# The residual x of the output projection, transposed by the transfer engines during the second branch's gates and kept in DRAM

## The chip, the cores and the metric

The kernel runs on one core of a Trainium2 chip. The metric is the device time of one execution in microseconds; less is better. The core has a matrix engine (TensorE, PE in the profile), a vector engine (VectorE, DVE), a scalar engine (ScalarE, ACT), a general engine (GpSimd, POOL), and SyncE (SP), which here only issues transfers. Transfers are carried out by 16 DMA engines.

## What is computed

One layer of a hybrid encoder, for 1024 prompt tokens and 32 sample tokens (1056 in all), width 1024, everything in 32-bit floats. Cut to what matters here:

```python
h = rmsnorm(x, norm_mix)
(a_b, a_c, a_x, qb, kb, vb, qc, kc, vc, qi, ki, wi, g_a, g_b, g_c) = split(h @ w_in)
br_a = (a_b * causal_dwconv(a_c * a_x)) @ w_a_out      # branch 1: gated convolution
br_b = window_attention(qb, kb, vb) @ w_swa_o          # branch 2
br_c = sparse_attention(qc, kc, vc, qi, ki, wi) @ w_dsa_o   # branch 3: top-k keys
merged = sigmoid(g_a) * br_a + sigmoid(g_b) * br_b + sigmoid(g_c) * br_c
x = x + merged @ w_out                                 # the residual that is changed
x = x + conv_ffn(rmsnorm(x, norm_ffn))                 # w_gate, w_up, w_down
y = rmsnorm(x, norm_final)
```

## The kernel before

Activations lie in SBUF with the channels on the 128 partitions and the 1056 tokens along the row ("columns"); a tile is 128 channels. To reach the accuracy of 32-bit floats, every matrix product is made of three products of rounded halves: high weights by high values, high weights by low values, low weights by high values. ACT makes the high part of a weight tile (`w_hi`, line 2240 is the helper that copies), DVE or POOL the low part (`w_lo`). A *job* is the product of one 128-column tile of weights with all tokens: 8 token tiles of nine matmuls each (line 1602), or 4 where the input is only 512 wide. The jobs are numbered in the order in which PE runs them; each uses one of two weight slots and one of two groups of PSUM banks, so the weights of job n are split when job n-2 is done.

All waits are written by hand with semaphores; each engine has its own instruction stream and runs it in order. SP's stream issues nearly all transfers, so a wait in it holds up every transfer behind it.

**The gates of the second branch** (jobs from `J_GB` on; `gate_loads` for SP, `gates` for ACT, DVE and PE). After the window attention, a loop of eight passes runs, two jobs a pass: a gate tile (8 token tiles; ACT takes its tanh, line 2466) and a tile of the branch's projection (4 token tiles). Beside them SP loads the gate weights of the third branch into `gate_w_raw`, ACT and POOL split them, and `gate_store` writes the two parts to DRAM, from where the sparse attention reads them later. In a pass SP waits for `lo_ready` before it loads w_in's tile for the gate job two ahead of the running ones, for `gate_lo` before `gate_store`, then loads the tile of w_swa_o, then the next `gate_w_raw`.

**The output projection** (jobs `J_WO` and `J_WO` + 1, then `out_product`). Before it, the eight jobs of the third branch's projection are merged: DVE multiplies with the gates, which lie where the residual will be (`GATES` and `X2` both start at SBUF unit 0), adds, and counts `sum_ready`; ACT and DVE make `merged_hi` and `merged_lo`. Output tiles 0 and 1 are plain jobs. Tiles 2 to 7 are made in three pairs by a scheme of seven half-sized products instead of eight (A11, S1, S2, S4, S3, A12, A22), each 24 matmuls of 264 columns (line 2009). They need sums and differences of quarters of the weights (`out_sum`, line 3653, DVE), their high parts (`out_hi`, ACT) and low parts (`out_lo`, line 3659, DVE), and mixes of the merged halves (`merged_mix`, lines 3620 to 3636, DVE; their high parts by ACT, line 2667). DVE adds each product to the residual `X2` (line 3668, `out_add`), for tiles 0 and 1 whole (line 3672, `residual`). PE waits for some of these additions before it starts a product in the same banks.

The residual has to be in columns, but x comes in rows. Before, SP loads x again in rows (`x_rows_again`, lines 1130 to 1133) when the third branch's last product is done, PE transposes it with 72 identity products (`x_tile`, eight after each of nine token tiles of jobs `J_WO` and `J_WO` + 1, into banks 6 and 7), and ACT evicts each set into `X2` (`xr_out`). DVE waits for all nine evictions ahead of `residual(0)`. Behind the loads of x, SP loads w_out's columns for pair 1 (line 1142), the second half of them once job `J_WO` + 1's weights are split.

## Time and profile before

| | us |
|---|---|
| median of the runs | 1749.39 |
| the runs | 1749.38, 1749.39, 1750.65 |
| span of the profiled execution | 1748.6 |
| PE busy | 1717.8 |
| DVE busy | 1341.5 |
| ACT busy | 757.8 |
| POOL busy | 579.4 |

The span goes from the first to the last instruction of one profiled execution; the median is of executions without the profiler, and lies 0.8 us above it. Starts in the rows below are microseconds from the start of that span. An instruction's duration includes its latency, so that the next one on the same engine can start a little before it ends: DVE's operations on 512 or 528 elements last 0.68 to 0.70 us and follow each other by 0.60 to 0.62, those on 1056 elements by 1.17.

### The profile page before, as it was taken

To read this page: it belongs to the slowest core of one execution; us is meant where nothing else is said; L and a number is where in the kernel's file an instruction comes from. 1 tells how busy PE (TensorE), PEld (TensorE's weight loads), DVE (VectorE), ACT (ScalarE), POOL (GpSimd) and SP (SyncE) were. 2 spreads that over 40 slices of the span, in tenths; PEclk is the share of its full clock that TensorE was granted. 3 is DMA by queue.
4 is the path that set the end of the run, shared out by engine and by line. 5 is a ranking of instruction groups with operands and counts; after the bars stand their busy time and mean duration, and the time that the engine had idled before them with its cause. 6 is when DMAs were issued, how large, how long until landed. Compare 5 with 4: busy or idle time off the path is not lost.

```text
span 1748.6 us, 32318 instructions
## 1 busy us (share of the span) xinstructions
PE 1717.8 (98%) x12275; PEld 1678.6 (96%) x12275; DVE 1341.5 (77%) x2193; ACT 757.8 (43%) x1333; POOL 579.4 (33%) x466
## 2 busy tenths in 40 slices
PE   6999999999999999999999999999999999999998
PEld 6999999999999999888899999999999999999998
DVE  6689899978799996778759989666666665865765
ACT  5344333368621234767734563333333333422334
POOL 2211842266745431000021102655455554121130
PEclk9999999999999999999999999999999999999999
DMA  4101111111243415422324112222222223533112
GB/s 157 49 25 43 49 43 48 49 38 28 68 137 124 128 40 171 144 85 85 109 71 151 49 49 61 87 85 75 74 80 80 87 74 111 167 117 112 61 37 100
DMA packets 179190, 146.43 MB, mean 84 GB/s; under 512 B 10140, under 2 KB 149676, under 8 KB 179052
## 3 DMA queue, kind: packets, MB, share of 16 engines
q1 hardware_dynamic: 178076, 142.54, 26.3%
q0 software_dynamic: 976, 2.00, 0.5%
q8 instruction: 93, 1.52, 0.4%
q14 instruction: 45, 0.37, 0.1%
HBM read 118.22 MB, written 26.28 MB: 83 GB/s over the span
## 4 chain that ended last, share of the span: by engine, by line
PE 91%; DVE 4%; ACT 2%; issue 1%; DMA 1%; POOL 1%; SPq 0%; DVEq 0%; ACTq 0%; POOLq 0%
PE ps L1602 28%; PE ps L2079 23%; PE ps L2152 7%; PE ps L2138 7%; PE ps L1714 5%; PE ps L1775 4%; PE ps L1795 4%; PE ps L1614 4%; PE ps L2009 3%; PE ps L1921 3%; PE ps L1869 1%; PE ps L1632 1%; PE ps L1876 1%; ACT probs L2537 0%; DMA x_rows<-in_x_prompt 0%
## 5 line engine op out<-in xcount | busy, mean ns | idle before, releaser
L3171 DVE MAX8 top<-key_mask 128x8 f32<-128x1024 f32 (+5 forms) x166 | 151.8, 917 | 9.7 <-DVE key_mask L3171 3.4
L1602 PE MATMUL ps<-h_hi,w_hi 128*128 128x352 f32 (+1 forms) x720 | 158.0, 327 | 0.0
L1602 PE MATMUL ps<-h_hi,w_lo 128*128 128x352 f32 (+1 forms) x720 | 155.2, 323 | 0.0
L1602 PE MATMUL ps<-h_lo,w_hi 128*128 128x352 f32 (+1 forms) x720 | 154.8, 323 | 0.0
L1289 POOL TENSOR_TENSOR w_lo<-w_raw,w_hi 128x512 fp32r<-128x512 f32 (+1 forms) x43 | 79.3, 1843 | 217.4 <-ACT w_hi L2240 217.3
L3171 DVE MATCH_REPLACE8 key_mask<-top,key_mask 128x1024 f32<-128x1024 f32 (+5 forms) x166 | 149.4, 904 | 0.3 <-issue 0.3
L2079 PE MATMUL ps<-mix_hi,quarter_hi 128*128 128x264 f32 x672 | 136.9, 285 | 0.2 <-ACT x_one L2240 0.2
L2079 PE MATMUL ps<-mix_hi,quarter_lo 128*128 128x264 f32 x672 | 136.4, 284 | 0.0
L2079 PE MATMUL ps<-mix_lo,quarter_hi 128*128 128x264 f32 x672 | 136.0, 284 | 0.0
L1602 PEld LDWEIGHTS ps<-h_hi,w_hi 128*128 128x128 f32 (+1 forms) x720 | 120.6, 187 | 2.6 <-issue 0.9
L1602 PEld LDWEIGHTS ps<-h_hi,w_lo 128*128 128x128 f32 (+1 forms) x720 | 122.5, 186 | 0.5
L1602 PEld LDWEIGHTS ps<-h_lo,w_hi 128*128 128x128 f32 (+1 forms) x720 | 121.5, 186 | 0.5
L2240 ACT ACTIVATE w_hi<-w_raw 128x1024 fp32r<-128x1024 f32 (+3 forms) x88 | 65.7, 749 | 125.6 <-PE ps L2138 56.5
L3800 DVE TENSOR_TENSOR quarter_lo<-sum,quarter_hi 128x512 fp32r<-128x512 f32 x84 | 71.1, 864 | 59.4 <-ACT quarter_hi L2240 59.1
L2079 PEld LDWEIGHTS ps<-mix_hi,quarter_hi 128*128 128x128 f32 x672 | 104.4, 189 | 0.6 <-ACT x_one L2240 0.4
L2079 PEld LDWEIGHTS ps<-mix_lo,quarter_hi 128*128 128x128 f32 x672 | 104.2, 188 | 0.0
L2079 PEld LDWEIGHTS ps<-mix_hi,quarter_lo 128*128 128x128 f32 x672 | 103.9, 188 | 0.0
L2079 PE MATMUL ps<-h_hi,quarter_lo 128*128 128x264 f32 x504 | 103.1, 286 | 0.0
L2079 PE MATMUL ps<-h_hi,quarter_hi 128*128 128x264 f32 x504 | 102.5, 285 | 0.6 <-ACT z_one L2240 0.6
L2079 PE MATMUL ps<-h_lo,quarter_hi 128*128 128x264 f32 x504 | 102.7, 285 | 0.0
L3512 DVE TENSOR_TENSOR probs_t_lo<-ps,probs_t_hi 128x512 fp32r<-128x512 f32 (+1 forms) x112 | 71.9, 642 | 33.1 <-ACT probs_t_hi L2240 32.0
L2240 ACT ACTIVATE quarter_hi<-sum 128x512 fp32r<-128x512 f32 x84 | 50.1, 626 | 89.7 <-POOL sum L1516 49.4
(452 smaller groups left out, 5017.5 us busy)
## 6 DMA issues: line engine op xcount, KB each, us to landing
w_raw<-in_w_in SPq DMA_DIRECT2D x54, 256.0 KB, 3.0
w_hi<-gate_highs SPq DMA_DIRECT2D x48, 256.0 KB, 2.8
w_lo<-gate_lows SPq DMA_DIRECT2D x48, 256.0 KB, 3.0
ffn_tiles<-t SPq DMA_DIRECT2D x44, 264.0 KB, 2.4
w_raw<-in_w_gate SPq DMA_DIRECT2D x44, 256.0 KB, 3.1
w_raw<-in_w_up SPq DMA_DIRECT2D x44, 256.0 KB, 3.1
w_raw_in_lo<-in_w_in SPq DMA_DIRECT2D x30, 256.0 KB, 3.0
w_raw<-in_w_down SPq DMA_DIRECT2D x32, 192.0 KB, 2.8
```

The costliest lines, as they stand in the source:

```text
L1289: nc.gpsimd.tensor_tensor(WLO[:, k, 0:tiles, :], raw[:, k, 0:tiles, :], WHI[:, k, 0:tiles, :].bitcast(F32), ALU.subtract).then_inc(lo_read ...
L1602: last = nc.tensor.matmul(PS[0:rows, NB * k + b, 0:e - a], w[:, k, t, 0:rows], x[:, t, a:e], start=m == 0 and w is WHI and x is hi, stop=m ...
L1614: last = nc.tensor.transpose(out, in_, IDENT[p0:p0 + r, p0:p0 + r])
L1714: last = nc.tensor.matmul(PS[:, 2 * bank + b, 0:QP], a_slot(w, n)[:, t, :], x[:, tile + t, at + b * QP:at + (b + 1) * QP], start=first and ...
L1775: last = nc.tensor.matmul(piece_bank(q), wt[:, w % 2, t, :], piece_at(x, t, p), start=t == 0 and wt is WHI and x is H_HI, stop=t == KT - 1 ...
L2079: last = nc.tensor.matmul(PS[:, 2 * pair + b, 0:QP], w[:, t * P:(t + 1) * P], x[:, tile + t, a:a + QP], start=first and t == 0 and w is WQ ...
L2138: last = nc.tensor.matmul(PS[:, NB * k + b, 0:PIECE], w[:, k, t, :], x[:, b * PIECE:(b + 1) * PIECE], start=t == 0 and w is WHI and x is F ...
L2152: last = nc.tensor.matmul(PS[:, 2 * pair + b, 0:QP], w[:, t * P:(t + 1) * P], x(t, b * QP, (b + 1) * QP), start=first and t == 0 and w is ...
L2240: return nc.scalar.activation(out, in_, ACT.Copy)
L3171: step.mark(V_.max(top, s) if find else V_.match_replace(s, top, s, TAKEN))
L3512: V_.tensor_tensor(PT_LO[:, q % 2, 0:n], PS[:, 4 + q % 2, 0:n], PT_HI[:, q % 2, 0:n].bitcast(F32), ALU.subtract).then_inc(pt_lo, 1)
L3800: V_.tensor_tensor(WQ_LO[q][:, :], src, WQ_HI[q][:, :].bitcast(F32), ALU.subtract).then_inc(q_lo_ready, 1)
```

## The change

The rows of x aren't loaded again. x, seen as 16-bit words, is a matrix with 2048 columns; channel c is its columns 2c and 2c + 1. In pass j of the gates loop SP issues two transposing transfers (prompt and sample) of 256 such columns, from DRAM into `X_TURNED`, 128 partitions by 2 by 1056 words; `x_bounce` writes that to DRAM so that each of the 256 columns is a row there; `x_plane_load` reads it back with the two halves of one channel in one partition (`X_PLANES`); ACT copies it so that the halves of each token lie side by side, which makes the 32-bit words of 128 channels of x in columns (`X_COLUMNS`); `x_store` writes this tile to DRAM. At the output projection SP waits for the last merge and for the stores, and loads the eight tiles straight into `X2`; DVE waits for them (two tiles a semaphore) before it adds. The transposes, the evictions and the waits for them go.

The diff, cut:

```diff
@@ SBUF and DRAM @@
-        XR = place("x_rows_again", [P, NT + 1, D], F32, 24)
+        X_TURNED = place("x_halves_turned", [P, 2, TOK], U16, 38)
+        X_PLANES = place("x_half_planes", [P, 2, TOK], U16, 39)
+        X_COLUMNS = place("x_columns", [P, TOK], F32, 40)
...
+        X_HALVES = nc.dram_tensor("x_halves", (2 * D, TOK), U16, kind="Internal").ap()
+        X_TILES = nc.dram_tensor("x_tiles", (KT, P, TOK), F32, kind="Internal").ap()
@@ SP @@
+            def x_turn(j):
+                at = bass.ds(j * (2 * P), 2 * P)
+                sp.dma_start_transpose(X_TURNED[:, :, 0:SEQ], x_halves(ins["x_prompt"])[:, at]).then_inc(xt_turned, 16)
+                sp.dma_start_transpose(X_TURNED[:, :, SEQ:TOK], x_halves(ins["x_sample"])[:, at]).then_inc(xt_turned, 16)
+            def x_bounce(j):
+                at = bass.ds(j * (2 * P), 2 * P)
+                sp.wait_ge(xt_turned, 32 * j + 32)
+                apart(sp)
+                sp.dma_start(X_HALVES[at, :].rearrange("(c p) t -> p c t", p=P), X_TURNED[:, :, :]).then_inc(xt_halves, 16)
+            def x_plane_load(j):
+                at = bass.ds(j * (2 * P), 2 * P)
+                sp.wait_ge(xt_halves, 16 * j + 16)
+                apart(sp)
+                sp.dma_start(X_PLANES[:, :, :], X_HALVES[at, :].rearrange("(p h) t -> p h t", h=2)).then_inc(xt_planes, 16)
+            def x_store(j):
+                sp.wait_ge(xt_columns, landed(j + 1))
+                apart(sp)
+                sp.dma_start(X_TILES[bass.ds(j, 1), :, :].rearrange("a p t -> p (a t)"), X_COLUMNS[:, :]).then_inc(xt_stored, 16)
@@ SP, gate_loads @@
                 sp.dma_start(GATE_RAW[:, :, :], columns(w_in, C_G + 2 * D)).then_inc(sparse_raw, 16)
+                sp.wait_ge(pv_done, WINDOW[-1]["q"] + len(WINDOW[-1]["chunks"]))
+                x_turn(0)
+                x_bounce(0)
+                x_plane_load(0)
                 with sp.Fori(1, KT) as j:
+                    x_turn(j)
                     free(n0, j, 0)
                     load(0, plain(0, w_in[:, :, bass.ds(j * P + (C_G + gate * D), P)]))
                     gate_store(j - 1)
+                    x_bounce(j)
+                    x_store(j - 1)
                     free(n0, j, 1)
                     load(1, split(j))
+                    x_plane_load(j)
                     sp.wait_ge(gates_stored, 32 * j)
@@ SP, attention_loads @@
                 if n0 == J_C:
+                    x_store(KT - 1)
                     gate_store(KT - 1)
@@ SP, output projection @@
             sp.wait_ge(job_done, J_WO - 1)
-            for i in range(0, NT, 2):
-                src = ins["x_prompt"][0, i * P:(i + 2) * P, :].rearrange("(t p) d -> p t d", p=P)
-                sp.dma_start(XR[:, i:i + 2, :], src).then_inc(xr_in[i // 2], 16)
-            sp.dma_start(XR[0:DEC, NT, :], x_rows(NT)).then_inc(xr_in[NT // 2], 16)
+            sp.wait_ge(sum_ready, KT)
+            sp.wait_ge(xt_stored, landed(16 * KT))
+            for j in range(KT):
+                sp.dma_start(X2[:, j, :], X_TILES[j]).then_inc(xr_in[j // 2], 16)
@@ PE @@
-            project(J_WO, 0, 0, M_HI, M_LO, ready=(m_lo, 0), order=SPARSE_ORDER,
-                    between={t: x_tile(t - 3) for t in range(3, KT)})
-            project(J_WO, 0, 1, M_HI, M_LO, between={t: x_tile(t + 5) for t in range(4)})
+            project(J_WO, 0, 0, M_HI, M_LO, ready=(m_lo, 0), order=SPARSE_ORDER)
+            project(J_WO, 0, 1, M_HI, M_LO)
...
-                if m == 1:
-                    pe.wait_ge(xr_out, NT + 1)
-                else:
+                if m > 1:
                     pe.wait_ge(added, out_count(1, Q_S4 if m == 2 else Q_A22))
@@ ACT, gates @@
                     following(n0, j, 1)
+                    act.wait_ge(xt_planes, landed(16 * j + 16))
+                    act.wait_ge(xt_stored, landed(16 * j))
+                    apart(act)
+                    copy(X_COLUMNS[:, :].bitcast(U16).rearrange("p (t h) -> p t h", h=2),
+                         X_PLANES[:, :, :].rearrange("p h t -> p t h")).then_inc(xt_columns, 1)
@@ ACT, attention_jobs @@
+                if n0 == J_C:
+                    act.wait_ge(xt_stored, landed(16 * KT))
@@ ACT, output projection @@
-            for i in range(NT + 1):
-                r = rows_of(i)
-                act.wait_ge(xr_t, i + 1)
-                src = PS[:, 6:8, :].rearrange("p b (j t) -> p (b j) t", t=P)
-                copy(X2[:, :, i * P:i * P + r], src[:, :, 0:r]).then_inc(xr_out, 1)
@@ DVE @@
+                if q in (Q_A11, Q_S1, Q_S2):
+                    dve.wait_ge(xr_in[m], 32)
...
                 done(J_WO, 0, k)
+                dve.wait_ge(xr_in[0], 32)
...
-            dve.wait_ge(xr_out, 5)
             mix_t_raw(4)
-            dve.wait_ge(xr_out, NT + 1)
```

## Rows read from the trace of the kernel before

**Rows 1.** The page's first part: busy us, share of the span, instructions.

```profile
PE 1717.8 (98%) x12275; PEld 1678.6 (96%) x12275; DVE 1341.5 (77%) x2193; ACT 757.8 (43%) x1333; POOL 579.4 (33%) x466
```

**Rows 2.** Instructions on x_rows_again: duration in ns min/median/max, first and last start.

```profile
L1614 PE MATMUL ps<-ident,x_rows_again x72: 221/272/273, 942.4 to 961.6; 128*128 128x128 f32 x64, 32*128 32x32 f32 x8
```

**Rows 3.** Timeline of PE: start us, us, line, operation, count [idle before <-releaser].

```profile
936.59 0.65 PE L1602 MATMUL ps<-merged_hi,w_hi 128*128 128x352 f32 x3
...
942.41 1.04 PE L1614 MATMUL ps<-ident,x_rows_again 128*128 128x128 f32 x8
...
967.64 0.41 PE L2009 MATMUL ps<-merged_hi,out_hi 128*128 128x264 f32 x2
```

**Rows 4.** Timeline of ACT, last eviction of x.

```profile
961.82 0.39 ACT L2240 ACTIVATE residual<-ps 128x256 f32<-128x256 f32 x1 [1.02 <-PE ps L1614]
```

**Rows 5.** Timeline of DVE from the last merge on.

```profile
938.23 1.26 DVE L3401 TENSOR_TENSOR conv_in<-merge_sum,t 128x1056 f32<-128x1056 f32 x1
...
953.67 0.68 DVE L3653 TENSOR_TENSOR out_sum<-w_raw 128x512 f32<-128x512 f32 x1
...
958.80 2.56 DVE L3636 TENSOR_TENSOR merged_mix<-merged_mix,merged_lo 128x528 f32<-128x528 f32 x4
...
962.24 1.26 DVE L3672 TENSOR_TENSOR residual<-ps,residual 128x1056 f32<-128x1056 f32 x1 [0.88 <-ACT residual L2240]
...
963.41 0.68 DVE L3659 TENSOR_TENSOR out_lo<-w_raw,out_hi 128x512 fp32r<-128x512 f32 x1
...
969.01 2.55 DVE L3623 TENSOR_TENSOR merged_mix_lo<-merged_mix,merged_mix_hi 128x528 fp32r<-128x528 f32 x2
...
982.46 0.71 DVE L3668 TENSOR_TENSOR residual<-ps,residual 128x528 f32<-128x528 f32 x1 [0.55 <-PE ps L2009]
```

**Rows 6.** Timelines of POOL and PE: differences of residual, a wait.

```profile
967.88 3.11 POOL L1497 TENSOR_TENSOR mix<-residual 128x528 f32<-128x528 f32 x2 [33.26 <-PE ps L1602]
...
994.43 0.51 PE L2009 MATMUL ps<-merged_mix_hi,out_hi 128*128 128x264 f32 x2 [0.30 <-DVE residual L3668]
```

**Rows 7.** SP's queue; stretches: length, busy PE PEld DVE ACT POOL, PEclk, DMA, GB/s.

```profile
936.79 2.08 SPq L1132 DMA_DIRECT2D x_rows_again<-in_x_prompt  x4
...
944.00:946.00 2.00, 2.00 (x17) 1.99 (x16) 1.83 (x4) 0.69 (x2) 0.00 (x0) 1.00 1.03 424
...
953.00:954.00 1.00, 1.00 (x8) 0.97 (x7) 1.00 (x3) 0.83 (x1) 0.00 (x0) 1.00 0.00 0
```

**Rows 8.** A stretch of the opening, columns as in rows 7.

```profile
16.00:20.00 4.00, 2.67 (x17) 2.46 (x17) 3.86 (x8) 2.66 (x4) 0.69 (x1) 0.68 0.78 180
```

**Rows 9.** Gates loop: a stretch as in rows 7, timelines of ACT, POOL, PE.

```profile
498.00:516.00 18.00, 18.00 (x113) 18.00 (x112) 16.58 (x26) 3.58 (x4) 8.54 (x4) 1.00 0.46 145
...
482.12 1.05 ACT L2240 ACTIVATE w_hi<-w_raw 128x1024 fp32r<-128x1024 f32 x1
...
486.92 0.63 ACT L2240 ACTIVATE w_hi<-w_raw 128x512 fp32r<-128x512 f32 x1 [3.75 <-PE ps L1602]
...
483.25 2.41 POOL L1289 TENSOR_TENSOR w_lo<-w_raw,w_hi 128x1024 fp32r<-128x1024 f32 x1 [6.58 <-ACT w_hi L2240]
...
486.72 0.65 PE L1602 MATMUL ps<-h_hi,w_hi 128*128 128x352 f32 x3
```

**Rows 10.** SP's queue, PE; issues with count, KB each, us to landing.

```profile
462.76 0.94 SPq L1007 DMA_DIRECT2D w_raw<-in_w_in  x2
...
468.87 0.28 PE L1921 MATMUL ps<-probs_t_lo,v_parts 128*128 128x256 f32 x1
...
gate_w_raw<-in_w_in SPq DMA_DIRECT2D x1, 512.0 KB, 3.8
...
gate_highs<-gate_w_hi SPq DMA_DIRECT2D x1, 512.0 KB, 2.7
```

**Rows 11.** Stretches as in rows 7: w_in's load; the store of idx_k_rows.

```profile
465.00:466.00 1.00, 1.00 (x10) 1.00 (x9) 0.00 (x0) 0.26 (x2) 1.00 (x2) 1.00 1.15 344
...
152.20:152.40 0.20, 0.20 (x4) 0.20 (x3) 0.20 (x1) 0.00 (x0) 0.00 (x0) 1.00 0.96 205
```

More of the change, by code:

```diff
@@ L1983, in _ @@
                 project(0, n // 2, n % 2, O_HI, O_LO, tiles=CT, pieces=ROUNDS)
-            def x_tile(i):
-                def run():
-                    pe.wait_ge(xr_in[i // 2], 16)
-                    pe.wait_ge(xr_out, i)
-                    r = rows_of(i)
-                    for j in range(KT):
-                        transpose(PS[:, 6 + j // 4, (j % 4) * P:(j % 4) * P + r],
-                                  XR[0:r, i, j * P:(j + 1) * P], xr_t if j == KT - 1 else None)
-                return run
-            project(J_WO, 0, 0, M_HI, M_LO, ready=(m_lo, 0), order=SPARSE_ORDER,
-                    between={t: x_tile(t - 3) for t in range(3, KT)})
-            project(J_WO, 0, 1, M_HI, M_LO, between={t: x_tile(t + 5) for t in range(4)})
+            project(J_WO, 0, 0, M_HI, M_LO, ready=(m_lo, 0), order=SPARSE_ORDER)
+            project(J_WO, 0, 1, M_HI, M_LO)
             def out_product(m, q, hi, lo, first=False, mix=None):
```

7 lines of the change are left out of this document (5 added, 2 removed).

## Prediction

> **What bounds the kernel now.** I read the page first. TensorE is busy 98% of the span [rows 1], so whatever takes time from PE with the other engines ready moves the end one for one, and so does whatever makes it wait. Busy shares can't tell which stretches have no second limit, so I read the two places the change touches: the output projection (936 to 994 us) in the timelines of PE, ACT, DVE and SP's queue, and the loop over the second branch's gates (461 to 606 us), where PE is busy 18.00 of every 18 us [rows 9].
>
> **Part 1: what leaves PE and ACT.** The 72 transposes of x [rows 2] go. They stand between groups of nine matmuls: the first four tiles of job 0 have none behind them and take 942.41 - 936.59 = 5.82 us, 1.455 each; jobs 0 and 1 together last from 936.59 to 967.64 = 31.05 us; sixteen tiles alone are 4 x 5.82 = 23.28 [rows 3]. PE loses 7.8 us and reaches the end of job 1 at 959.9. That is the ceiling, 0.44% of the span. ACT's nine evictions of x go too; ACT idled ahead of each, 1.02 us before the last [rows 4].
>
> **Part 2: DVE takes over.** The first product after job 1 (A11 of pair 1) needs its low weights (line 3659). In DVE's timeline its work from the merges on is an unbroken string up to 958.80 + 2.56 = 961.36; then 0.88 us of waiting for ACT's last eviction, residual(0) at 962.24, low weights at 963.41 [rows 5]. None of this string waits for the transposes except those 0.88 us, and DVE loses no instruction. Freed, it starts residual(0) at 961.36 and finishes A11's low part at 961.36 + 1.17 + 0.68 = 963.2: PE, there at 959.9, idles 3.3 us. Further on: PE needs A11's addition (line 3668) before product S2. DVE does from 963.2: low S1 0.60, five mixes 3.1, residual(1) 1.17, two mixes 1.2, low S2 0.60, the addition 0.69 = 970.6, and 1.2 us more where POOL's differences double the mixes behind residual(1) (969.01: 2.55 for two, while at 958.80 four of that size took 2.56; POOL's pair began at 967.88) [rows 5, 6]: 971.9. S2 could start then at best, against 973.5 before (967.64 and two products of 2.93 us). The same string holds PE today: at 994.43, before S2 of pair 2, it waited 0.30 us for an addition of DVE [rows 6], and from 945 to there DVE idled 0.88 and 0.55 us only (the second ends at 982.46) [rows 5]. So of the 7.8 us at most 0.88 + 0.55 + some tenths, 1.5 to 2.3 us, can come through. After 994 DVE waits for PE again; what is left there is kept.
>
> **Part 3: the late loads take that back.** The x loads went out from 936.79 on, w_out's for pair 1 behind them on the same queue, which ran at 424 GB/s with DMA share 1.03 and was empty by 953 [rows 7]: 4.3 MB of x and 1.05 MB of weights. DVE's weight sums (line 3653) began at 953.67, some 0.8 us later. The changed loads write over the gates, so SP waits for the last merge: 938.23 + 1.26 = 939.49 [rows 5]. They go out at 939.6, 2.8 us later, with the same bytes; the weights land near 955.7. DVE, ready at 953.67, waits 2.0 us. Residual(0) starts at 961.36 + 2.0 = 963.4 instead of 962.24, PE idles 959.9 to 965.3 (5.4 us), the chain arrives at 982 some 1.1 us late, the 0.55 us wait there absorbs half, and S2 of pair 2 starts about 0.5 us later than 994.43. Term of this stage: **+0.5 us**, bounds -2.3 (loads hidden) and +1.5 (the stored tiles flow a tenth slower than x's rows). The new waits of DVE for x tiles 0 and 1 end near 944 and cost nothing.
>
> **The clock in that gap.** In the opening, where PE was busy 2.67 of 4 us, its granted clock was 0.68 in the mean, so part of that stretch ran at the lower level, 1.2 GHz [rows 8]. A gap of 5.4 us may do the same: a product of 2.93 us (24 matmuls of 264 columns) would take 5.9 then. But S2 waits for DVE until about 973.9, while A11 and S1 need PE to 971.2 only, so 2.7 us of it are covered; I add nothing to the likeliest case, up to 1.5 us to the range. The Trainium skill (TensorE: Matmul & The Clock Gate, "Why this matters for your kernels") says that an idle gap between bursts puts the clock back to its lower level; the opening of this trace agrees.
>
> **Part 4: the gates loop.** Each of eight passes gains two transposing loads of together 540 KB, a store, a load and a store of 540 KB each, and an ACT copy. The copy has 2 x 1056 elements, at 1.05 us for 1024 [rows 9] 2.1 us; ACT idles 3.75 us before its next split [rows 9]: 0. The traffic, 2.16 MB in a pass of twelve tiles (12 x 1.455 = 17.46 us), adds 124 to 145 GB/s; the DMA share is 0.46 [rows 9]: 0 by itself. What counts is SP's order. The new wait for the last product of the window attention stands ahead of everything from pass 1 on. That product runs at 468.87 and ends by 469.2; today w_in's load for pass 1 leaves at 462.76 [rows 10]. Call X the time in which 540 KB flow transposed. From 469.25: fixed part of a load 2.3 (3.8 for gate_w_raw's 512 KB [rows 10] less 1.5 at 344 GB/s [rows 11]), X, the small second load 0.3: turned at 471.85 + X. Store 2.7 (gate_highs' landing [rows 10]): 474.6 + X. The plane load takes 2.0 to flow and 1.4 in flow: 478 + X; the next pass's transposes stand behind it until 478 + 2X, then w_in's 512 KB, 1.5: **479.5 + 2X**. ACT wants it at 482.12, POOL's 2.41 us end at 485.66, PE wants it at 486.72: 1.06 us spare, so due at 483.15 [rows 9, 10]. PE loses 2X - 3.65. X is not in this trace. From below: 1.3 us at the 424 GB/s of x's rows [rows 7] and 1.6 at the 344 of w_in's 512-byte pieces [rows 11]: no loss. The store of idx_k_rows, in 256-byte pieces, ran at 205 [rows 11]; if a transpose reads 128 columns of 16 bits at a time, its pieces are as long: X = 2.6, loss 1.6 us. From above: 205 GB/s is 20 ns for each such piece on one of 16 engines; if it were cut into 32-byte pieces (16 tokens of one column), X = 17,000 x 20 ns / 16 = 21 us. I take 2.6, the row with the nearest pieces: **+1.6 us**.
>
> The Trainium skill (Advanced Engine Details and Errata, "X-Bar Transpose (TRN2)") has transposing loads as fast as others, 350 to 400 GB/s; DMA: Bandwidth & Descriptors, "Latency and other measured facts", has 261 GB/s with a non-contiguous middle dimension. X would be 1.5 or 2.1 and this term 0 or 0.5, an estimate from those pages; no run here shows it yet.
>
> From pass 2 on SP waits for ACT's copy, 4.1 us after the tanh (split 2.0, copy 2.1), before w_b's load, whose job starts 11.6 us later (0). Then plane load (issued 7.0 after the tanh), gate_w_raw, transposes and w_in queue up: 7.0 + 2.0 + 1.4 + 1.5 + X + 1.5 + 0.5, due 17.46 + 2.0 after it: hidden up to X = 5.6. The last x_store holds up gate_store and the next attention's ACT, both of whose readers come a job of 11.6 us later: 0.
>
> **Sum.** The profiled span is 1748.6, 0.8 us under the median of the runs, 1749.39. 1749.4 + 0.5 + 1.6 = **1751.4**.
>
> **Rivals.** (a) Transposes are slow: X above 3.3 us makes the first pass lose over 3 us, with the +0.5 over 0.2%. X = 4.5 gives 5.4 + 0.5: 1755.3. For it: the small pieces, the 21 us above. Against: the rows at 344 and 205. Chance 0.27 for X up to 5.6. (a') Slower still: X = 7 gives 10.4 in the first pass and 7 x 1.4 = 9.8 in the others: 1770; 0.13. (b) They flow like plain loads, X under 1.7, and the w_out loads are late: +0.5, 1749.9. 0.15. At 350 to 400 GB/s the Trainium skill's page (Advanced Engine Details and Errata) leads here. (c) The loads of part 3 are hidden too, DVE's string alone bounds: 1749.4 - 2.0 = 1747.4; 0.08. (d) DVE doesn't bind and the whole 7.8 comes through: 1741.6; against it stands the unbroken string. 0.05. The likeliest case, X from 1.7 to 3.3, holds 0.32; its own range is 1749.5 to 1753.
>
> **How the numbers follow.** A measurement of this kernel can tell about 0.2%, 3.5 us, from no change. Faster 0.05; slower 0.40; within 0.55. The range leaves out (d), most of (c), and X above 6: low 1748.0, high 1762 (X = 5.8: 8.0 + 1.4 + 0.5 + clock 1.5 = 1760.8, rounded up).
>
> **What would show it.** Right: PE idle some 5 us before line 2009's first product, DVE idle 2 us before line 3653, residual(0) at the same distance from the last merge as worked out; PE idle at the third job of the gates loop only, for w_lo of that job, and ACT's w_hi there waiting for a DMA; transposes landing 4.5 to 5.5 us after issue. Wrong: a PE gap at the projection under 3 us (part 3), landings over 6 us or a gap in each pass (part 4), or a clock below 1.00 for longer than the gap. A stall of PE in another stage would overthrow the sum.

## The result, and the profile after

The changed kernel takes 1756.84 us, the median of five runs (1756.74 to 1758.49), where the kernel before took 1749.86 beside it: a ratio of 1.0039, interval 1.0028 to 1.0049. The change makes the kernel some 7 us slower. The forecast was 1751.4 in a range of 1748.0 to 1762.0; the range held, the likeliest case (1749.5 to 1753) did not. The time and a loss of over 3 us in the first pass of the gates loop are those of rival (a); whether its reason held too is asked further down.

First the page's first part and the opening of its second, to be read against [rows 1]:

```profile
span 1755.0 us, 32315 instructions
PE 1713.7 (98%) x12203; PEld 1674.2 (95%) x12203; DVE 1344.6 (77%) x2193; ACT 766.5 (44%) x1332; POOL 583.6 (33%) x466
```

PE lost its 72 instructions and 4.1 us of busy time, and the span grew by 6.4 us. ACT has 8.7 us more (eight copies of 2.2 us less nine evictions). So PE must wait longer. The list of PE's waits says where (waiting engine and line, what it waited for: us in total, times, longest):

```profile
PE ps L2043 <- DVE out_lo L3693: 6.1, 1, 6.1
PE ps L1647 <- POOL w_lo L1334: 4.2, 1, 4.2
PE ps L2043 <- DVE residual L3704: 0.8, 2, 0.5
```

The first and the second are new, the third was one of 0.3 us [rows 6]; the others differ from those of before by 0.1 us. The first stands in the output projection and takes the place of the transposes, the second in the gates loop.

**The gates loop.** SP's queue from the end of the window attention on, then ACT, POOL and PE (start us, us, engine, line, operation, count, idle before and releaser):

```profile
469.26 2.37 SPq L1068 DMA_TRANSPOSE x_halves_turned<-in_x_prompt  x1
471.69 1.49 SPq L1069 DMA_TRANSPOSE x_halves_turned<-in_x_sample  x1
475.24 0.39 SPq L1076 DMA_DIRECT2D x_halves<-x_halves_turned  x1
478.13 0.35 SPq L1083 DMA_DIRECT2D x_half_planes<-x_halves  x1
478.69 3.35 SPq L1068 DMA_TRANSPOSE x_halves_turned<-in_x_prompt  x1
482.09 1.23 SPq L1069 DMA_TRANSPOSE x_halves_turned<-in_x_sample  x1
483.66 1.04 SPq L1017 DMA_DIRECT2D w_raw<-in_w_in  x2
...
487.54 1.06 ACT L2272 ACTIVATE w_hi<-w_raw 128x1024 fp32r<-128x1024 f32 x1 [5.23 <-DMA w_raw<-in_w_in]
...
488.67 2.35 POOL L1334 TENSOR_TENSOR w_lo<-w_raw,w_hi 128x1024 fp32r<-128x1024 f32 x1 [11.93 <-ACT w_hi L2272]
...
491.16 1.19 PE L1647 MATMUL ps<-h_hi,w_hi 128*128 128x352 f32 x3 [4.20 <-POOL w_lo L1334]
...
495.70 0.65 PE L1647 MATMUL ps<-h_hi,w_hi 128*128 128x352 f32 x3
```

It is the forecast chain: wait for the window product, turn, bounce, plane load, the next pass's turns, w_in. The load leaves at 483.66 instead of 462.76 [rows 10], ACT starts the split 5.4 us later than in [rows 9], and PE's job starts at 491.16 instead of 486.72. What the rows show besides: a transposing transfer holds SP's queue while it is being issued, 2.37 and 1.49 us here, 3.35 and 1.23 in the next pass. Behind the gap, in stretches of PE (length, busy PE, PEld, DVE, ACT, POOL, granted clock, DMA share, GB/s):

```profile
490.00:491.00 1.00, 0.00 (x0) 0.00 (x0) 1.00 (x2) 0.69 (x1) 1.00 (x1) 1.00 0.66 256
...
492.00:493.00 1.00, 1.00 (x5) 1.00 (x4) 0.89 (x2) 0.00 (x0) 0.00 (x0) 0.50 1.03 410
...
495.00:496.00 1.00, 1.00 (x8) 1.00 (x7) 1.00 (x3) 0.59 (x1) 0.00 (x0) 1.00 0.83 300
```

PE idles at the full clock, and the clock falls to its lower level, 1.2 GHz, just as the work resumes: five matmuls a microsecond instead of eight, for 3.4 us. What that costs can be read between the first matmuls of the job's token tiles 0 and 2. In the kernel before the second of these is

```profile
489.64 0.65 PE L1602 MATMUL ps<-h_hi,w_hi 128*128 128x352 f32 x3
```

2.92 us behind the job's start at 486.72 [rows 9]; in the kernel after it is at 495.70, 4.54 us behind 491.16. The slow clock costs 1.62 us. The last merge, which started at 938.23 [rows 5], starts at 944.17. Of these 5.94 us, 4.44 are there when the job starts and 1.62 come behind it from the clock; the small rest is within the scatter of this distance (below).

**The output projection.** DVE and PE:

```profile
962.46 0.69 DVE L3687 TENSOR_TENSOR out_sum<-w_raw 128x512 f32<-128x512 f32 x1 [2.77 <-DMA w_raw<-in_w_out]
...
970.07 1.25 DVE L3709 TENSOR_TENSOR residual<-ps,residual 128x1056 f32<-128x1056 f32 x1
...
972.06 0.78 PE L2043 MATMUL ps<-merged_hi,out_hi 128*128 128x264 f32 x2 [6.10 <-DVE out_lo L3693]
...
980.42 0.52 PE L2043 MATMUL ps<-merged_mix_hi,out_hi 128*128 128x264 f32 x2 [0.54 <-DVE residual L3704]
...
1001.44 0.51 PE L2043 MATMUL ps<-merged_mix_hi,out_hi 128*128 128x264 f32 x2 [0.30 <-DVE residual L3704]
```

The last row answers to the one at 994.43 [rows 6]: 7.01 us later, so 1.07 us were lost in this stage. PE gained the transposes' 7.8 us and spent them, and a little more, waiting and at the lower clock.

**A measure for the experiments.** Two distances in each profile part the stages: the start of the last merge (it holds what the gates loop cost), and from there to the start of S2 of pair 2 (what the projection cost). What follows is PE's alone. Worked out from the timelines of DVE and PE of each profiled execution:

| kernel | last merge starts | to S2 of pair 2 | from there to the last matmul | to the span's end |
|---|---|---|---|---|
| before | 938.23 | 56.20 | 746.93 | 7.2 |
| after | 944.17 | 57.27 | 746.97 | 6.6 |
| gates_only | 944.03 | 56.22 | 745.32 | 8.5 |
| projection_only | 937.98 | 57.14 | 745.34 | 7.5 |
| first_load | 938.71 | 57.21 | 746.95 | 6.6 |
| weights_first | 943.76 | 54.42 | 746.96 | 6.6 |
| plain_turn | 941.97 | 57.19 | 746.97 | 6.6 |
| both_orders | 939.01 | 54.42 | 746.97 | 6.6 |
| both_less_mix | 938.93 | 53.87 | 747.00 | 6.6 |
| pool_sums | 939.31 | 58.86 | 746.95 | 6.6 |
| late_pieces | 939.02 | 55.98 | 746.96 | 6.6 |
| first_square | 937.63 | 55.12 | 746.94 | 6.6 |
| square_late_sum | 939.62 | 54.51 | 746.99 | 6.7 |
| filled_waits | 937.57 | 53.59 | 747.23 | 6.6 |

The second distance repeats to 0.1 us in kernels that share the projection (57.14 to 57.27; 54.42 twice). The first scatters by 2 us among the seven kernels from both_orders on, which are the same up to there. What follows S2 of pair 2, the last two columns together, scatters by 1.3 among all fourteen. So a single span says little about 1 us, and the second distance says it well.

### The profile page after: what moved, and what is told of

It reads as the page before. It is cut to its first block, busy times and chain, and to the rows that moved or that the text cites. A ratio compares the mean times of both kernels' runs of the same rounds, so it can differ in the third digit from the quotient of the medians.

```text
span 1755.0 us, 32315 instructions
## 1 busy us (share of the span) xinstructions
PE 1713.7 (98%) x12203; PEld 1674.2 (95%) x12203; DVE 1344.6 (77%) x2193; ACT 766.5 (44%) x1332; POOL 583.6 (33%) x466
## 4 chain that ended last, share of the span: by engine, by line
PE 84%; DVE 6%; issue 3%; ACT 3%; POOL 2%; DMA 2%; SPq 0%; DVEq 0%; ACTq 0%; POOLq 0%
PE ps L1647 25%; PE ps L2111 23%; PE ps L2184 7%; PE ps L2170 7%; PE ps L1820 4%; PE ps L1840 4%; PE ps L1659 3%; PE ps L1966 2%; PE ps L2043 2%; PE ps L1759 2%; PE ps L1914 1%; PE ps L1677 1%; PE ps L1921 1%; POOL w_lo L1377 1%; POOL w_raw_in_lo L1390 1%
```

## The experiments

The first four part the change by place, the fifth by what the transfers cost, the rest ask what bounds the projection.

**gates_only**: the kernel before with the changed gates loop; the projection is that of before.

```diff
@@ on the kernel after @@
-            sp.wait_ge(sum_ready, KT)
-            sp.wait_ge(xt_stored, landed(16 * KT))
-            for j in range(KT):
-                sp.dma_start(X2[:, j, :], X_TILES[j]).then_inc(xr_in[j // 2], 16)
+            for i in range(0, NT, 2):
+                src = ins["x_prompt"][0, i * P:(i + 2) * P, :].rearrange("(t p) d -> p t d", p=P)
+                sp.dma_start(XR[:, i:i + 2, :], src).then_inc(xr_in[i // 2], 16)
...
-            project(J_WO, 0, 1, M_HI, M_LO)
+            project(J_WO, 0, 1, M_HI, M_LO, between={t: x_tile(t + 5) for t in range(4)})
```

> The kernel before with the gates loop of the changed one: x is turned, bounced, put together and stored, but nobody reads it; the projection keeps its 72 transposes. My theory (two separate costs: SP's order in the first pass of the gates loop, 5.9 us with the clock's fall, and 1.1 us at the projection): 1755.8, 1755 to 1756.5, one PE gap of about 4 us ahead of the third job of the loop. Rival (the stored tiles, their late loads and the projection cost most of it): under 1752.

Measured: 1756.15 us beside 1750.74, ratio 1.0036, interval 1.0022 to 1.005. PE's wait in the gates loop:

```profile
490.78 0.86 PE L1649 MATMUL ps<-h_hi,w_hi 128*128 128x352 f32 x3 [4.13 <-POOL w_lo L1336]
```

The last merge comes 5.80 us late, and the projection is that of before (56.22). Nearly the whole loss of the change is in the gates loop.

**projection_only**: the change without its gates loop; the tiles of x are loaded from the bytes of a weight, so that it isn't x that is added.

```diff
-                sp.dma_start(X2[:, j, :], X_TILES[j]).then_inc(xr_in[j // 2], 16)
+                sp.dma_start(X2[:, j, :], STAND_IN[j]).then_inc(xr_in[j // 2], 16)
```

> The changed projection without the gates loop's part: the eight tiles are loaded into the residual from w_down's bytes as a stand-in, so the residual is wrong; times of the loads are the same. My theory: 1751.0, 1750.3 to 1751.6; PE gap of 5 to 6 us ahead of the first half-sized product, DVE waits 2 to 3 us for w_out. Rival (what is lost at the projection comes from the shift by the gates loop): faster than before by 2 us or more.

Measured: 1750.51 us, ratio 1.0, interval 0.9991 to 1.0009. PE's gap:

```profile
965.76 0.78 PE L2007 MATMUL ps<-merged_hi,out_hi 128*128 128x264 f32 x2 [5.99 <-DVE out_lo L3650]
```

The gap is there without any loss ahead of it, and the stage is 0.94 us longer (57.14). 7.8 us less work on PE give nothing. That the time shows no loss either doesn't speak against it: the interval holds 0.94 us, and in the profiled execution the end came 1.3 us sooner behind S2 of pair 2 than in the kernel before.

**first_load**: the change, with pass 1's first load of w_in ahead of the new wait and of the first turns.

```diff
+                gate_tile(1)
                 sp.wait_ge(pv_done, WINDOW[-1]["q"] + len(WINDOW[-1]["chunks"]))
                 x_turn(0)
```

> The changed kernel with one transfer moved: w_in's tile for pass 1 is loaded ahead of the wait for the window attention and of the first turn. My theory (only that load is late): PE's gap in the gates loop goes, 1751.0, 1750.3 to 1751.8. Rival (the doubled traffic or ACT's copy slows the passes): the gap moves to another weight tile, 1754 or more.

Measured: 1750.76 us, ratio 1.0, interval 0.9991 to 1.0009. The load and the first turn on SP's queue:

```profile
462.23 1.07 SPq L1017 DMA_DIRECT2D w_raw<-in_w_in  x2
468.98 2.02 SPq L1068 DMA_TRANSPOSE x_halves_turned<-in_x_prompt  x1
```

PE no longer waits in the gates loop, with all the traffic, all the copies and all later passes as they were. One load moved ahead of the wait takes back the 6 us. So the loss was the order of issue in one pass; the bandwidth and ACT's copies cost nothing that shows.

**weights_first**: the change, with pair 1's tiles of w_out ahead of six of the eight x tiles.

```diff
-            for j in range(KT):
-                sp.dma_start(X2[:, j, :], X_TILES[j]).then_inc(xr_in[j // 2], 16)
+            x_loads(range(2))
...
+                if m == 1:
+                    x_loads(range(2, KT))
```

> The changed kernel with w_out's loads for pair 1 put behind x tiles 0 and 1 and ahead of tiles 2 to 7. My theory (DVE's own string bounds the projection, the late w_out load adds its wait): DVE's wait of 2.8 us goes, PE's gap falls from 6.1 to about 3.3 us and stays there, 1754.0, 1753.2 to 1754.6. Rival (late loads are the whole of the lost gain): the gap goes, 1750.5 or less. Rival (another wait takes its place, for x tiles 2 and 3): 1755.5 or more.

Measured: 1754.42 us, ratio 1.0022, interval 1.0013 to 1.0031.

```profile
968.79 0.48 PE L2048 MATMUL ps<-merged_hi,out_hi 128*128 128x264 f32 x2 [3.24 <-DVE out_lo L3698]
977.16 0.51 PE L2048 MATMUL ps<-merged_mix_hi,out_hi 128*128 128x264 f32 x2 [0.75 <-DVE residual L3709]
```

DVE doesn't wait for w_out any more, PE's gap is 3.24 us, and the stage takes 54.42: 2.85 less than after, 1.78 less than before. This is what the transposes were worth once the loads are out of the way.

**plain_turn**: the change, with each pair of transposing transfers replaced by three plain ones of as many bytes; what is turned isn't x, and another tensor is added in its place.

```diff
-                sp.dma_start_transpose(X_TURNED[:, :, 0:SEQ], x_halves(ins["x_prompt"])[:, at]).then_inc(xt_turned, 16)
+                for h in range(2):
+                    rows = x_halves(ins["x_prompt"])[h * 512:(h + 1) * 512, at].rearrange("(c p) n -> p c n", p=P)
+                    sp.dma_start(X_TURNED[:, h, 0:SEQ].rearrange("p (c n) -> p c n", n=2 * P), rows).then_inc(xt_turned, 16)
```

> The changed kernel with its two transposing transfers of a pass replaced by three plain ones of as many bytes (two of 512 KB together in 512-byte pieces, one small one); every wait, the bounce through DRAM, the ScalarE copy, the stores and the place of each load on SP's queue stay. What is turned is then not x, so the projection adds another tensor as x (read from a weight's bytes), and that part of the result is left wrong. Theory 1 (it is what a transposing transfer costs beyond its bytes, in flow and above all in issue on SP's queue, that makes pass 1's first w_in load late): SP is through with each pair of turns in under 2 us instead of 3.9 to 6.2, the first w_in load of pass 1 is issued near 478 instead of 483.66, TensorE's wait of 4.2 us for its low halves falls to 0.5 us or less, and the time is 0.7 to 1.5 us over the kernel before, near 1751.0 where that is 1750.0. Rival (the new wait and the two round trips ahead of the load are enough, however fast a turn is): TensorE still waits 2 us or more in the gates loop and the time stays 4 us or more over the kernel before, 1754 or later.

Measured: 1752.4 us beside 1750.62, ratio 1.0011, interval 1.0002 to 1.002. SP's queue and PE:

```profile
468.96 0.92 SPq L1071 DMA_DIRECT2D x_halves_turned<-in_x_prompt  x2
469.92 0.51 SPq L1073 DMA_DIRECT2D x_halves_turned<-in_x_prompt  x1
474.45 0.39 SPq L1080 DMA_DIRECT2D x_halves<-x_halves_turned  x1
...
477.92 0.95 SPq L1071 DMA_DIRECT2D x_halves_turned<-in_x_prompt  x2
...
479.75 0.93 SPq L1018 DMA_DIRECT2D w_raw<-in_w_in  x2
...
488.69 0.74 PE L1651 MATMUL ps<-h_hi,w_hi 128*128 128x352 f32 x3 [2.04 <-POOL w_lo L1338]
```

Both sides missed: theory 1 wanted a gap of 0.5 us or less, the rival had the gap (2 us or more) but wanted 1754 or later. From the first issue to the store of what was turned it takes 5.49 us here and 5.98 with transposes: the transposing itself costs half a microsecond. The second pair costs more: from its first issue to that of w_in 1.83 us here, 4.97 there, since SP issues no other transfer meanwhile. 1.4 us of those 3.1 are given back, since ACT has w_in's data only 5.31 us after the issue, at 485.06, instead of 3.88, in the flow of the turn ahead of it. So of the 4.2 us, 2.2 are the transposing transfers (1.7 of it their issue), and 2.0 are the wait and the round trips, which plain transfers pay too. A gap of half the length cost the same in clock: the last merge starts 3.74 us late, 1.97 of it there at the gap's end, and the job's first three tiles take 6.01 us instead of 4.38, 1.63 from the clock. These figures are of one execution, and it was the slowest of the eleven (1754.46, the median is 1752.4). The median lies only 1.8 us above the kernel before, so most executions lost less in this loop than this one; how long PE waited in them isn't known.

**both_orders**: first_load and weights_first together (both diffs above).

> The changed kernel with both orders of issue mended: pass 1's first w_in load ahead of the wait for the window product and of the first turns, and the first pair of w_out's tiles ahead of the x tiles 2 to 7. Theory 1 (the two losses are separate, so their savings add, and VectorE's string is what is left): no wait of TensorE in the gates loop, 3.2 to 3.3 us of wait ahead of the first half-sized product with VectorE never waiting for w_out, that product pair's end about 2 us earlier than in the kernel before, and a time 1.2 to 2.2 us under it, a ratio of 0.9988 to 0.9993, near 1748.2 where the kernel before takes 1750.0. Rival (what is won in one place is lost in the other, or the end takes it): ratio at 1.0 or above.

Measured: 1748.78 us beside 1750.62, ratio 0.9988, interval 0.9979 to 0.9997. 1.8 us faster than the kernel before, and, by the two ratios, some 9 us faster than after. PE waits 3.26 us for DVE, and the stage takes 54.42, as in weights_first to the hundredth. Around the gap:

```profile
962.00:964.00 2.00, 0.00 (x0) 0.00 (x0) 2.00 (x4) 2.00 (x5) 0.55 (x1) 1.00 0.00 0
...
966.00:968.00 2.00, 2.00 (x11) 2.00 (x10) 2.00 (x4) 0.71 (x1) 2.00 (x1) 0.50 0.00 0
```

DVE is busy in both without a break. The clock falls behind the gap here too, for 3.4 us between 965 and 969, but PE is then ahead of DVE and waits for it again at 972.41, 0.74 us: the slow stretch is covered.

**both_less_mix**: both_orders, with the second step of the fourth mix on 32 of its 528 columns, so that operand lacks the rest of its low-order part.

```diff
-                    V_.tensor_tensor(T_RAW[d][t][:, :], T_RAW[d][t][:, :], M_LO[:, tile + t, 0:HALF].bitcast(F32),
+                    n = 32 if d == 4 else HALF
+                    V_.tensor_tensor(T_RAW[d][t][:, 0:n], T_RAW[d][t][:, 0:n], M_LO[:, tile + t, 0:n].bitcast(F32),
```

> The kernel with both orders mended, and in it VectorE's second step of the fourth mix (four additions of 528 columns, 2.55 us in all) done on 32 of the 528 columns alone, so that this part of one operand, and with it the result, is wrong. Theory 1 (VectorE's unbroken string of work from the last merge to the first low halves of w_out is what TensorE waits for): the wait shrinks by what the string loses, from 3.2 us to 1.0 to 1.3, and the time falls by another 2 to 3 us, to 0.9975 to 0.998 of the kernel before. Rival (TensorE waits for something else that ends at the same time, such as ScalarE's high halves of w_out or its evictions): the wait stays at 3 us or more and the time at that of both orders.

Measured: 1747.56 us, ratio 0.9979, interval 0.997 to 0.9988.

```profile
961.90 0.48 PE L2057 MATMUL ps<-merged_hi,out_hi 128*128 128x264 f32 x2 [1.19 <-DVE out_lo L3708]
970.25 0.51 PE L2057 MATMUL ps<-merged_mix_hi,out_hi 128*128 128x264 f32 x2 [2.22 <-DVE residual L3719]
```

A stretch behind the second of these rows:

```profile
972.00:974.00 2.00, 2.00 (x11) 2.00 (x11) 2.00 (x5) 0.00 (x0) 0.00 (x0) 0.50 0.03 8
```

DVE's string binds: 2.1 us less of it, and the first gap is 2.07 us shorter, the second products start 2.16 earlier. But the stage is only 0.55 us shorter. The first products now ran at the full clock, PE had 2.22 us to wait ahead of S2, and the clock fell behind that wait, where nothing covers it: from S2 of pair 1 to that of pair 2 PE needs 22.55 us instead of 21.02. Theory 1 had the gap right. Of its 2 to 3 us the stage gave 0.55, since the clock took 1.5 us; the medians differ by 1.2 us. The ratio of 0.9979 lies in its range of 0.9975 to 0.998, and the interval is too wide to tell the two amounts apart.

**pool_sums**: both_orders, with the four sums of w_out's quarters for pair 1 on GpSimd.

```diff
+                nc.gpsimd.tensor_tensor(out_source(1, q), x, y, op).then_inc(pair_sum, 1)
...
-            out_weights(1, *SUMS)
```

> The kernel with both orders mended, and the four sums of w_out's quarters for pair 1 (4 x 0.66 us on VectorE, ahead of its low halves) made by GpSimd instead, which has nothing to do between 940 and 968. The result stays whole. Theory 1 (VectorE's string binds, and GpSimd's sums at about 1.3 us each, done near 961, are off the path): TensorE's wait ahead of the first half-sized product falls from 3.2 us to 0.5 to 1.0 us, and the time to 0.9970 to 0.9978 of the kernel before, near 1745.5 where that is 1750.0. Rival (VectorE and GpSimd slow each other while both run, or GpSimd's last sum makes the high halves of the sums late): the wait stays over 2 us, or a new one of over 1 us stands ahead of S1, S2 or S4, and the time is no better than with both orders alone.

Measured: 1753.06 us, ratio 1.001, interval 1.0001 to 1.0019. GpSimd, ACT, DVE and PE:

```profile
952.01 8.93 POOL L1557 TENSOR_TENSOR out_sum<-w_raw 128x512 f32<-128x512 f32 x1 [16.32 <-DMA w_raw<-in_w_out]
961.01 1.68 POOL L1557 TENSOR_TENSOR out_sum<-out_sum,w_raw 128x512 f32<-128x512 f32 x1
...
960.97 0.63 ACT L2296 ACTIVATE out_hi<-out_sum 128x512 fp32r<-128x512 f32 x1 [10.80 <-POOL out_sum L1557]
...
963.16 6.53 DVE L3678 SCALAR_TENSOR_TENSOR merged_mix_lo<-merged_mix,merged_mix_hi 128x528 fp32r<-128x528 f32 x5
...
961.68 0.49 PE L2067 MATMUL ps<-merged_hi,out_hi 128*128 128x264 f32 x2 [0.60 <-DVE out_lo L3717]
974.47 0.81 PE L2067 MATMUL ps<-merged_mix_hi,out_hi 128*128 128x264 f32 x2 [6.17 <-DVE residual L3728]
```

The first gap shrank to 0.60 us as theory 1 had it, and the rival took the gain and more. The first sum lasted 8.93 us, through DVE's string of two-operand work, the next ones 1.6 to 1.8, and ACT waited for it 10.8 us with nine high halves of the mixes queued behind. DVE was slowed in turn: beside GpSimd's later work its low half of S1 lasted 1.61 us instead of 0.68, and the five mixes of the row above 6.53 instead of 3.18 with both orders. Its addition for S2 came late, and PE waited 6.17 us for it, with the clock at 0.50 until 980. The stage takes 58.86. The Trainium skill (SBUF — State Buffer, "SBUF: two separate sides") says that DVE and GpSimd take turns at one pair of ports, locked for a whole instruction, also where DVE reads two operands from SBUF beside a GpSimd instruction that reads SBUF. This trace agrees, with 8.93 us for 1.7 us of GpSimd's work and 6.53 for 3.2 of DVE's.

**late_pieces**: both_orders, with the clearing of the sum of squares and the last of the four sums moved behind DVE's first addition to the residual (the clearing well behind it, after the third).

```diff
-            V_.memset(T0[:, 0:TOK], 0.0).then_inc(ssq_sum, 1)
...
-            out_weights(1, *SUMS)
+            out_weights(1, Q_S1, Q_S2, Q_S4)
...
             out_add(1, Q_A11)
+            out_weights(1, Q_S3)
...
+            V_.memset(T0[:, 0:TOK], 0.0).then_inc(ssq_sum, 1)
```

> The kernel with both orders mended, in which two pieces of VectorE's string are moved behind its first addition of a half-sized product to the residual, and none is taken away: the clearing of the sum of squares (0.87 us) and the last of the four sums of w_out's quarters (0.6 us). Theory 1 (VectorE binds through the whole stage, from the last merge to the third group of products at about 993, where it hardly idles, so work moved within it only moves the wait): the first wait shrinks from 3.3 to 1.8 us and the second product's wait for the residual ends 1.5 us earlier, but by 993 no more than 0.5 us of it is left, and the time is that of both orders alone, 0.9985 to 0.9990 of the kernel before. Rival (only the string up to the first addition binds): all of the 1.5 us comes through, and the ratio is 0.9978 to 0.9981.

Measured: 1750.37 us beside 1750.79, ratio 0.9995, interval 0.9986 to 1.0004. The first wait is 1.82 us, the second 2.25, and three more appear: 0.68, 0.69, 1.23 us. The stage takes 55.98, 1.56 more than with both orders. It is worse than either side expected. ACT's first square waits for the clearing by the code, and starts at 980.06 instead of 965.64; w_out's first high half for pair 2, queued behind it, starts at 983.51 instead of 981.94. So one of the two pieces was moved too far, and the run doesn't test theory 1 cleanly.

**first_square**: both_orders, with ACT's first square written straight into the sum, so that DVE neither clears it nor adds to it.

```diff
-                nc.scalar.activation(tokens(T1[:, 0:TOK]), tile_at(X2, j), ACT.Square).then_inc(res_sq, 1)
+                nc.scalar.activation(tokens((T1 if j else T0)[:, 0:TOK]), tile_at(X2, j), ACT.Square).then_inc(res_sq, 1)
...
-            V_.memset(T0[:, 0:TOK], 0.0).then_inc(ssq_sum, 1)
+            V_.memset(T0[:, 0:2], 0.0).then_inc(ssq_sum, 1)
...
+                if j == 0:
+                    V_.memset(T1[:, 0:2], 0.0).then_inc(ssq_sum, 1)
+                    return
```

> The kernel with both orders mended, in which 2.0 us of VectorE's work in this stage is done away with and the result stays whole: ScalarE writes its first square straight into the sum of squares, so VectorE neither clears it (0.87 us, ahead of the first half-sized product) nor adds that square (1.17 us, near 980). Theory 1 (VectorE binds through the whole stage): the first wait shrinks from 3.3 to 2.4 us, the second product's start is 0.9 us earlier, and so is the third group at 993.4, which keeps at least 0.5 us of it; ratio 0.9979 to 0.9986. Rival (TensorE's own work from 972 on is what counts, so VectorE's later work is hidden anyway and the clock dip takes what the first wait gave): ratio as with both orders alone, 0.9988 or above.

Measured: 1747.79 us beside 1750.79, ratio 0.9982, interval 0.9973 to 0.9991. The time lies where theory 1 had it, but the stage doesn't: it takes 55.12, 0.70 more than with both orders.

```profile
961.85 0.48 PE L2057 MATMUL ps<-merged_hi,out_hi 128*128 128x264 f32 x2 [2.42 <-DVE out_lo L3707]
970.20 0.56 PE L2057 MATMUL ps<-merged_mix_hi,out_hi 128*128 128x264 f32 x2 [2.25 <-DVE residual L3718]
```

and a stretch behind the second:

```profile
972.00:974.00 2.00, 2.00 (x11) 2.00 (x10) 2.00 (x4) 0.00 (x0) 0.00 (x0) 0.52 0.00 0
```

The first wait is 0.84 us shorter, the clock then held through the first products and fell behind the second wait instead. In this profile the rival's mechanism is what happened, though its ratio (0.9988 or above) is not. The better time came from ahead of the stage (last merge at 937.63) and lies within the interval of both_orders.

**square_late_sum**: first_square with the last of the four sums moved too.

```diff
-            out_weights(1, *SUMS)
+            out_weights(1, Q_S1, Q_S2, Q_S4)
```

> As the kernel that writes the first square straight into the sum, and the last of the four sums of w_out's quarters moved behind VectorE's first addition to the residual (0.6 us). Theory 1: the first wait is 1.8 us, the second product starts 1.5 us earlier than with both orders alone, and the ratio is 0.9976 to 0.9984, since the string has lost 2.0 us in all and what was only moved has room. Rival (a shorter first wait gives TensorE a wait later, with the clock falling where it counts, as where part of the fourth mix was left out): the second wait grows by 1 us or more, low clock stands behind it, and the ratio is 0.9985 or above.

Measured: 1747.85 us, ratio 0.9982, interval 0.9973 to 0.9991. The first wait is 1.82 us, the second 2.24 (0.74 with both orders), and the clock is 0.50 from 972 to 974 behind it; the stage takes 54.51. The second wait grew by 1.5 us with low clock behind it, as the rival had it. The ratio lies in theory 1's range, and the interval reaches the rival's too.

**filled_waits**: first_square, with 18 and 16 matmuls that nobody reads in PE's two waits.

```diff
+                if m == 1:
+                    fill(6, 18)
                     pe.wait_ge(taken[0], evicted(J_WO))
...
+                if m == 1:
+                    fill(2, 16)
                 pe.wait_ge(added, out_count(m, Q_A11))
```

> The kernel that writes the first square straight into the sum, in which TensorE fills its two waits of the output projection with products that nobody reads: 18 matmuls of 264 columns (some 2.2 us at full speed) ahead of the first half-sized product, 16 (some 2.0 us) ahead of the second pair of products. Nothing of the result changes. Theory 1 (what the waits cost beyond themselves is the lower clock behind them: without the fill, TensorE waits 2.25 us and then runs at half the clock from about 970 to 974, which makes the stretch from there to the third group 22.55 us long instead of 21.02): the granted clock stays at 1.00 from 958 to 980, the low rows go, and the third group starts 53.4 to 53.9 us after the last merge's start instead of 55.1; ratio 0.9970 to 0.9982. Rival (the low clock hangs on something else than TensorE's idling, or the fill delays the products it precedes by as much as it saves): the distance stays at 54.4 us or more, and the ratio at 0.9985 or above.

Measured: 1747.47 us beside 1750.56, ratio 0.9984, interval 0.9975 to 0.9993.

```profile
959.19 2.34 PE L2072 MATMUL ps<-merged_hi 128*128 128x264 f32 x18
961.79 0.49 PE L2057 MATMUL ps<-merged_hi,out_hi 128*128 128x264 f32 x2 [0.26 <-DVE out_lo L3714]
...
970.15 0.51 PE L2057 MATMUL ps<-merged_mix_hi,out_hi 128*128 128x264 f32 x2 [0.32 <-DVE residual L3725]
```

The stretch that answers to the low ones above:

```profile
970.00:972.00 2.00, 1.85 (x15) 1.85 (x16) 2.00 (x5) 0.00 (x0) 0.00 (x0) 1.00 0.03 8
```

The clock stays at 1.00 from 956 to 976, the two products start when they did, and the stage takes 53.59: 1.53 us less than first_square, which is just the excess of 22.55 over 21.02. So the low clock hangs on PE's idling, and it costs 1.5 us where nothing covers it. The time itself doesn't tell the two kernels apart: the stage came out in theory 1's range, while the ratio lies just above its 0.9970 to 0.9982 and just under the rival's 0.9985.

## Why the prediction came out as it did

**What binds** (parts 1 and 2): right. The 7.8 us came off PE; DVE's string took their place. The bare gap was put at 3.3 us; with the weights' wait gone it is 3.24 and 3.26. At most 1.5 to 2.3 us were to come through; in weights_first 1.78 did. The part's second bound, DVE's addition ahead of S2, held too: S2 was to start at 971.9 at best, 33.7 us behind the last merge, and in both_orders it starts 33.4 behind it. What the part doesn't draw from it is that a shorter first gap alone only lengthens the wait at the second bound.

**The late loads** (part 3): right in kind, a little small. From the last merge's start, w_out's data was due after 17.5 us (955.7 less 938.23) and came after 18.3; DVE's wait was 2.77 for 2.0, residual(0) came after 25.9 for 25.2, PE's gap was 6.10 for 5.4; with the order mended the stage got 2.85 us shorter. It lost 1.07 us against the +0.5 of the sum, inside the bounds of -2.3 to +1.5. The bytes flowed no slower than in [rows 7]. A stretch of the kernel after, in which the flow ends:

```profile
960.50:961.00 0.50, 0.50 (x5) 0.50 (x4) 0.00 (x0) 0.00 (x0) 0.00 (x0) 1.00 0.37 93
```

DVE, idle by then, began at 962.46, some 1.6 us behind it. I had taken the end of the flow ("empty by 953") for the landing; DVE was busy then in the kernel before and couldn't show the difference. So the term that was sized too small is the landing of w_out, by 0.8 us.

**The clock in the projection's gap**: right to add nothing. It was 0.50 from 970 to 974 in the kernel after, and low for 6.8 us in all, and PE still came early enough to wait 0.54 us ahead of S2 at 980.42. A clock below 1.00 for longer than the gap had been named as a sign of being wrong. It came (6.8 against 6.10) and cost nothing here: S2 was where DVE let it be.

**The gates loop** (part 4): the place, the queue's order, the landing that was late, and that only the first pass would lose were right. The term was +1.6 and measured +5.9, in three pieces. First X: by the formula, what was turned at 475.24 makes X 3.4 instead of 2.6; it counts twice, 1.6 us. Second, the rest of w_in's way: by 479.5 + 2X the data was due at 486.3 and ACT had it at 487.54, 1.2 us. Third, the clock behind the gap, 1.6 us, which I had thought of in the projection, where it was covered, and not here, where PE has no slack at all. 1.6 + 1.6 + 1.2 + 1.6 = 6.0, for 5.94 measured.

The step that failed is the meaning of X. I took it for a time of flow and set its bounds by bandwidth rows; the experiment with plain transfers shows that the flow is hardly different (5.49 against 5.98 us for the whole turn) and that it is SP's time of issue, 2.4 to 5.0 us for a prompt part and 1.2 to 1.5 for a sample part, that pushes the load behind. Read by the same formula, the plain turn's 5.49 us are an X of 2.9 and, since it began 0.3 us earlier, a loss of 1.8 us, where PE's job came 2.0 late; the assumed 2.6 was near for plain transfers of these pieces, and the rows at 344 and 424 GB/s were too hopeful as a bound from below. No row of before shows a transposing issue, and I let [rows 10] stand for it, where two plain ones take 0.94 us. The sign named for a wrong part 4, landings over 6 us, came: the prompt parts landed after 5.7 to 7.0 us, 6.2 in the median, where 4.5 to 5.5 was forecast. That the later passes hide their transfers held. The Trainium skill (Advanced Engine Details and Errata, "X-Bar Transpose (TRN2)") has such transfers as fast as others; the trace agrees to half a microsecond in 5.5, and yet rival (b), no loss in this loop, fell: plain transfers lost 3.7 us of it in their profiled execution too.

**Sum.** 5.94 (gates) + 1.07 (projection) = 7.01 us at S2 of pair 2 and 7.05 at the last matmul; the end gave 0.6 back in the profiled execution, 6.4 for the span, and the medians differ by 7.0. Against the forecast 2.1 these are 4.3 us too little in one term and 0.6 in the other. The price of rival (a), 5.4 + 0.5, was near, by luck: it argued from small pieces that flow slowly, with X = 4.5, where X by the formula was 3.4, and w_in's late landing and the clock made up the rest. That the range held owes something to the same luck, since its upper end was made of larger X and of a clock term thought of for the projection.

## What to carry to other kernels

When work is put on a queue, look first at what the queue issued early: a new wait placed ahead of a prefetch turns it into a load on demand. Here one load moved ahead of the wait was worth 6 us, far more than what the bandwidth or the copies cost. Taking work from the engine that is busy 98% of the time gains only what the next engine's string leaves, so follow that string to each place where the first engine waits for it, not to the first one only. And price an idle gap with the slow clock behind it: 1.5 to 1.6 us more here if nothing waits afterwards, nothing if the engine would have waited anyway, which also means that a shorter gap can make a stage longer.

## What the runs showed of the hardware

A transposing transfer occupies its issuing queue for microseconds (1024 tokens by 256 words of 16 bits: 1.9 to 5.2 us over all runs; 32 tokens: 1.2 to 1.9); most plain ones of 256 to 528 KB beside it take 0.3 to 0.6. The row is that of SP's instructions on x_halves_turned in the kernel after (duration in ns, min/median/max):

```profile
L1068 SPq DMA_TRANSPOSE x_halves_turned<-in_x_prompt x8: 2372/4069/4963, 469.3 to 582.8; - x8
L1069 SPq DMA_TRANSPOSE x_halves_turned<-in_x_sample x8: 1220/1220/1492, 471.7 to 587.0; - x8
```

Why the same issue takes 2.4 us in one pass and 5.0 in another wasn't tried; the shortest is that of the first pass, with the queue empty.

After most gaps of 2.0 to 6.2 us in the two places the clock fell to 0.50, and stayed there while PE was fully busy again: for 3.4 us with gaps of 2.0 to 4.2, for 6.8 with those near 6.0, and for 10.2 in pool_sums (6.17). In gaps up to 4.2 us it is still 1.00 in the idle stretch. The cost behind a gap of 2.04 us (1.63) was no less than behind one of 4.20 (1.62). Gaps of 1.19 and 1.82 us left it at 1.00, but so did one of 2.42 us, the first in first_square, and one of 2.25 in late_pieces, where another of 2.25, the second in first_square, didn't. What tells these apart wasn't tried.

The clock can also fall in the last transposes of the kernel, where PE idles only 0.4 us, between matmuls of a single column. From S2 of pair 2 to the last matmul it takes 746.9 to 747.2 us in the twelve kernels where it fell and 745.3 in the two where it didn't, in the same code. The kernel after:

```profile
1742.00:1745.00 3.00, 3.00 (x20) 2.68 (x20) 2.00 (x6) 1.11 (x1) 0.00 (x0) 0.68 0.35 143
```

and the one with the gates loop alone changed:

```profile
1739.00:1742.00 3.00, 3.00 (x29) 2.87 (x29) 1.94 (x7) 1.02 (x1) 1.16 (x1) 1.00 0.43 175
```

What decides it stays open, and the 1.6 us don't reach the span's end as they are. From S2 of pair 2 to there it takes 753.8 and 752.9 us in the two kernels where the clock held, 753.6 in the kernel after and 754.2 in the one before, since the last matmul is followed by 8.5 and 7.5 us where the clock held and by 6.6 to 7.2 elsewhere. The 1.3 us between these are as large as some of the effects looked for here.
